# The output gate's product moved into the recurrence, and a new order of the projection's tiles

## The reference, cut to what matters

```python
z = h @ w_in + b_in
q, k, v, o, gt, ga, gb = jnp.split(z, IN_SPLITS, axis=-1)   # 256, 256, 512, 512, 16, 512, 512 wide
u = ga * jax.nn.sigmoid(gb)                                 # goes into a 31-tap convolution
...
s = jnp.einsum('bhctk,bhcsk->bhcts', qc, kc) * jnp.exp(log_d - m_t[..., None])
num = (jnp.einsum('bhcts,bhcsv->bhctv', s, vc)
       + e_int[..., None] * jnp.einsum('bhcvk,bhctk->bhctv', C_prev, qc))
h = num / jnp.maximum(jnp.abs(den), jnp.exp(-m_t))[..., None]
...
hn = h * lax.rsqrt(jnp.mean(h * h, axis=-1, keepdims=True) + EPS) * norm_g
return hn * jax.nn.sigmoid(o)                               # for the tokens alone, not the context
```

## Time and profile before

| what | value |
|---|---|
| time, median of 3 runs | 3131.33 us (3129.58 to 3132.32) |
| profiled execution: its time / its span | 3128.74 us / 3127.0 us |
| granted TensorE clock over the span | 0.915 of full |
| busy over the span | PE 2696.8 us, DVE 1746.7 us, ACT 1241.8 us, POOL 1042.4 us |

### The profile page before, as it was taken

One profiled execution on the slowest core, in us unless ns is written; L12 is line 12 of the kernel. 1 busy time (PEld: TensorE's weight loads), 2 busy tenths in 40 slices (PEclk: granted clock), 3 DMA queues, 4 the chain that ended last, 5 costly groups with the idle time before them and its releaser, 6 DMA issues. The chain is left out here.

```text
span 3127.0 us, 39919 instructions
## 1 busy us (share of the span) xinstructions
PE 2696.8 (86%) x12102; PEld 1960.0 (63%) x12103; DVE 1746.7 (56%) x2591; ACT 1241.8 (40%) x1753; POOL 1042.4 (33%) x1119
## 2 busy tenths in 40 slices
PE   5999989787679999999999939958968999965997
PEld 2455446574267877777777737745745666754776
DVE  3767767654266678677786624545462111445663
ACT  2320124520055567566665623236122111215653
POOL 0860022124444445454453421384120000105432
PEclk8999975797789999999999979979989999977999
DMA  6430010323268789899898655000202111326972
GB/s 247 148 138 1 27 54 1 139 81 131 85 230 283 241 282 318 268 311 312 268 343 253 206 159 171 7 28 2 43 14 61 41 41 42 148 115 214 311 231 46
DMA packets 162929, 472.13 MB, mean 151 GB/s; under 512 B 38637, under 2 KB 67937, under 8 KB 142073
## 3 DMA queue, kind: packets, MB, share of 16 engines
q1 hardware_dynamic: 116576, 358.25, 30.5%
q0 software_dynamic: 44704, 108.22, 15.1%
q10 hardware_dynamic: 1544, 4.33, 0.3%
HBM read 419.82 MB, written 95.81 MB: 165 GB/s over the span
## 5 line engine op out<-in xcount | busy, mean ns | idle before, releaser
L1830 PE MATMUL psum<-moe_high,moe_xg_high 128*128 128x512 f32 x960 | 390.6, 407 | 21.8 <-DVE moe_xg_low L1925 11.8
L1832 PE MATMUL psum<-moe_high,moe_xg_low 128*128 128x512 f32 x960 | 378.7, 394 | 0.0
L1831 PE MATMUL psum<-moe_low,moe_xg_high 128*128 128x512 f32 x960 | 376.1, 392 | 0.0
L1920 DVE TENSOR_TENSOR moe_low<-moe_raw,moe_high 128x2048 fp32r<-128x2048 f32 x160 | 359.2, 2286 | 13.1 <-ACT moe_high L1865 12.9
L1865 ACT ACTIVATE moe_high<-moe_raw 128x2048 fp32r<-128x2048 f32 x160 | 297.8, 1917 | 0.2 <-DMA moe_raw<-in_w_e_up 0.2
L1817 PE MATMUL psum<-moe_high_down,moe_hid_high 128*128 x488 | 204.4, 419 | 41.7 <-DVE moe_hid_low L1935 41.6
L1830 PEld LDWEIGHTS psum<-moe_high,moe_xg_high 128*128 128x128 f32 x960 | 182.1, 190 | 59.2 <-issue 24.8
L1832 PEld LDWEIGHTS psum<-moe_high,moe_xg_low 128*128 128x128 f32 x960 | 181.3, 189 | 43.1
L1831 PEld LDWEIGHTS psum<-moe_low,moe_xg_high 128*128 128x128 f32 x960 | 182.2, 190 | 36.1
L1877 ACT ACTIVATE moe_y_blk<-psum,row_w 128x1024 f32 x124 | 138.0, 1113 | 143.9 <-PE psum L1819 143.9
L1761 POOL DMA_INDIRECT moe_second<-moe_y_blk,moe_is_now x48 | 120.8, 2517 | 219.5 <-ACT moe_y_blk L1877 215.5
(11 more groups left out here) (599 smaller groups left out, 5625.1 us busy)
## 6 DMA issues: line engine op xcount, KB each, us to landing
moe_raw<-in_we_gate SPq DMA_DIRECT2D x64, 1024.0 KB
moe_raw<-in_we_up SPq DMA_DIRECT2D x64, 1024.0 KB
moe_raw<-in_we_down SPq DMA_DIRECT2D x64, 1024.0 KB
x<-in_w_ada POOLq DMA_DIRECT2D x16, 1024.0 KB
moe_raw<-in_w_e_gate SPq DMA_DIRECT2D x16, 1024.0 KB
moe_raw<-in_w_e_up SPq DMA_DIRECT2D x16, 1024.0 KB
moe_raw<-in_w_e_down SPq DMA_DIRECT2D x16, 1024.0 KB, 8.6
w_ring<-in_w_in SPq DMA_DIRECT2D x12, 1024.0 KB, 8.6
```

The lines of the kernel that those rows point to most:

```text
L1830: pe.matmul(to, x_hi, R(of_k(w_hi, k)), start=(k == 0), stop=False)
L1831: pe.matmul(to, x_hi, R(of_k(w_lo, k)), start=False, stop=False)
L1832: last = pe.matmul(to, x_lo, R(of_k(w_hi, k)), start=False, stop=(k == KD - 1))
L1920: dve.tensor_tensor(R(low[:, at:at + 2048]), raw[r][:, part], hi, ALU.subtract).then_inc(w_low, 1)
```

## The change

1. The eight `o` tiles leave the projection's plan, and with them DVE's eight additions of the bias and ACT's eight sigmoids there.
2. In the recurrence PE makes the same product in pieces, `gate_product(i)`, i = 0 to 63: one K slice of one `o` tile behind each pair's numerator and one at each pair's end. A tile thus takes four pairs and lies in bank 7. The bias is a ninth product at each tile's start (one row of ones by `b_o`). ACT copies the finished tile out (`move_gate`) and PE starts the next one behind that copy.
3. Since bank 7 is taken, the state's contribution goes to bank 1, and both scores products go to bank 0. The second waits until the first has finished, and is laid between the numerator's two products.
4. The sigmoid of `o` is taken in `stage_mix`, ahead of the silu; DVE's scaling waits for it tile by tile.
5. The projection's plan is new: all `gb`/`ga` tiles come early, mixed with `qk` and `ada`, then `gt`, and the `v` tiles last with the `gate` steps between them. `upad` is doubled, so a `ga` tile waits only for the taps of the group before the last.
6. The squares of the convolution's output go to `s.x` in place of `s.hT`, since `hT` is still needed.

```diff
 def project_plan():
     gab = lambda m, between=(): [("gb", m, 0), ("ga", m, 0), *between, ("gb", m, 1), ("ga", m, 1)]
-    plan = gab(0) + [None]
-    for i in range(0, 8, 2):
-        plan += qk[i:i + 2] + [None]
...
-    plan += [("o", t, 0) for t in range(NT)] + [("kt", t, 0) for t in range(STEPS)]
+    plan = gab(0) + [None] + qk[0:2] + [None] + gab(1, [None]) + [None] + qk[2:5] + [None] + gab(2, [None]) + qk[5:6] + [None]
+    plan += gab(3, [None]) + qk[6:] + tile("gt", *range(NT)) + tile("v", NT, NT + 1) + tile("gt", NT, NT + 1)
+    for t in range(NT):
+        plan += tile("v", t) + (tile("gate", t - 1) if 1 <= t < 5 else [])
+    plan += tile("kt", *range(STEPS))
...
-                        taps(TAPS)
+                        taps(TAPS * (n_sig // 2 - 1) - taps_done)
...
-    s.upad, s.y = sb("upad", [P, ROWS, GRID + 2 * PAD]), sb("conv_y", [P, KC, T])
+    s.upad, s.y = sb("upad", [P, 2, ROWS, GRID + 2 * PAD]), sb("conv_y", [P, KC, T])
...
+                def scores(v, i):
+                    if i == 1:
+                        pe.wait_ge(scores_done, 2 * v + 1)
+                    pe.matmul(s.bank[0][:, i * P:(i + 1) * P], s.qkT[lanes(i), 2 + k, t0:t0 + P], s.qkT[lanes(i), k, t0:t0 + P],
+                              start=True, stop=True).then_inc(scores_done, 1)
+
+                def gate_product(i):
+                    t, k = divmod(i, KD)
+                    if k == 0:
+                        if t == 0:
+                            pe.wait_ge(s.mixer_weights.ready["o"], 32)
+                        else:
+                            pe.wait_ge(o_moved, t)
+                        pe.matmul(s.bank[7][:, :], s.ones[0:1, :], s.b_o[:, :], start=True, stop=False)
+                    last = pe.matmul(s.bank[7][:, :], s.hT[:, k, t * P:(t + 1) * P], w_o[:, k], start=False, stop=(k == KD - 1))
+                    if k == KD - 1:
+                        last.then_inc(o_done, 1)
...
                         pe.wait_ge(pt_ready, v + 1)
-                        if v + 1 < NV:
-                            scores(v + 1)
                         for i in range(2):
+                            if v + 1 < NV:
+                                scores(v + 1, i)
                             last = pe.matmul(s.bank[bank + i][:, 0:W], pt[:, v % 2, i, :], s.v_aug[:, tile_of(j, d), 2 * k + i, :],
                                              start=True, stop=True)
                         last.then_inc(num_done, 1)
+                        gate_product(2 * v)
...
                         last.then_inc(local_done, 1)
+                    if v >= 0:
+                        gate_product(2 * v + 1)
...
+                def move_gate(t):
+                    act.wait_ge(o_done, t + 1)
+                    act.activation(s.sig_o[:, t, :], s.bank[7], ACT.Copy).then_inc(o_moved, 1)
...
+            for t in range(NT):
+                act.activation(s.sig_o[:, t, :], s.sig_o[:, t, :], ACT.Sigmoid).then_inc(sig_ready, 1)
```

More of the change, by code:

```diff
@@ L441, in project_plan @@
     gab = lambda m, between=(): [("gb", m, 0), ("ga", m, 0), *between, ("gb", m, 1), ("ga", m, 1)]
-    last = [entry for i, part in enumerate((("gb", 3, 0), ("ga", 3, 0), ("gb", 3, 1), ("ga", 3, 1))) for entry in (part, ("gate", i, 0))]
-    v = lambda t0, t1: [(kind, t, 0) for t in range(t0, t1) for kind in ("v", "gt")]
     qk = [("qk", m, n) for n in range(3) for m in range(4) if n < 2 or m >= 2]
-    plan = gab(0) + [None]
-    for i in range(0, 8, 2):
-        plan += qk[i:i + 2] + [None]
-    plan += qk[8:] + gab(1, [None]) + v(0, 1) + [None] + v(1, 3) + [None] + v(3, STEPS // 2) + gab(2) + v(STEPS // 2, STEPS) + last
-    plan += [("o", t, 0) for t in range(NT)] + [("kt", t, 0) for t in range(STEPS)]
+    tile = lambda kind, *tiles: [(kind, t, 0) for t in tiles]
+    plan = gab(0) + [None] + qk[0:2] + [None] + gab(1, [None]) + [None] + qk[2:5] + [None] + gab(2, [None]) + qk[5:6] + [None]
[3 more added lines that the diff above has]
+    plan += tile("kt", *range(STEPS))
     places = [i for i, entry in enumerate(plan) if entry is None]
@@ L508, in _ @@
                         pe.wait_ge(moved_a if plan[i - 8][0] in by_act else moved_v, place[i - 8])
-                    if kind in ("qk", "v", "gt", "o") and i == first[kind]:
+                    if kind in ("qk", "v", "gt") and i == first[kind]:
                         pe.wait_ge(w_ready[kind], 16 if kind == "gt" else 32)
@@ L553, in taps @@
                         w = s.convw[:, tap * KC + m:tap * KC + m + 1]
-                        rows, to = s.upad[:, :, tap:tap + GRID], s.y[:, m, :].rearrange("p (r w) -> p r w", w=GRID)
+                        rows, to = s.upad[:, m % 2, :, tap:tap + GRID], s.y[:, m, :].rearrange("p (r w) -> p r w", w=GRID)
                         if tap == 0:
@@ L587, in _ @@
                         moved = dve.tensor_tensor(s.gates[:, a, :], bank[:, 0:N_GT], b_gt[:, 0, :], ALU.add)
-                    elif kind == "o":
-                        if i == first["o"]:
-                            dve.wait_ge(later.added, 2 * later.KH * later.TILES)
-                        c.then(dve.tensor_tensor(s.sig_o[:, a, :], bank[:, :], b_o, ALU.add))
-                        c.wait(dve)
-                        moved = dve.sem_inc(moved_v, 1)
-                        dve.sem_inc(o_added, 1)
-                        continue
                     else:
@@ L611, in _ @@
                         gates.logs(dve)
-                taps(TAPS)
+                taps(TAPS * KC)
                 dve.wait_ge(gates.exps_ready, 4)
@@ L624, in _ @@
                         gates.scalar_exps(act)
-                    if kind == "o":
-                        act.wait_ge(o_added, a + 1)
-                        s.act_c.then(act.activation(s.sig_o[:, a, :], s.sig_o[:, a, :], ACT.Sigmoid))
                     if kind not in by_act:
@@ L647, in _ @@
                 c.then(pool.memset(s.v_aug[:, :, :, DV:DV + 1], 1.0))
-                pool.memset(s.upad[:, :, :], 0.0).then_inc(pads_set, 1)
+                pool.memset(s.upad[:, :, :, :], 0.0).then_inc(pads_set, 1)
                 later.load(pool)
@@ L824, in stage_mlstm @@
     N, INVERT, SCALE = 512, 0, 2 * KC + 4
-    sqy = s.hT[:, 0:KC, :]
+    sqy = s.x[:, NT // 2:NT, :]
+    w_o = s.mixer_weights.ring[:, 1]
+    local = s.bank[1][:, 0:W]
     s.rstd_y = s.hcT.rearrange("p k c -> p (k c)")[:, 1024:1024 + T]
@@ L843, in stage_mlstm @@
         y_inv, y_root, y_done, out_done = (sem(s, f"y_{x}") for x in ("inv", "root", "done", "out_done"))
+        o_done, o_moved = sem(s, "m_o_done"), sem(s, "m_o_moved")
         sq = sb("m_sq", [P, P])
@@ L882, in maxima @@
                     last.then_inc(maxima_done, 1)
-                def scores(v):
+                def scores(v, i):
                     j, d, k = pairs[P0 + v]
                     t0 = tile_of(j, d) * P
-                    for i in range(2):
-                        last = pe.matmul(s.bank[i][:, 0:P], s.qkT[lanes(i), 2 + k, t0:t0 + P], s.qkT[lanes(i), k, t0:t0 + P],
-                                         start=True, stop=True)
-                    last.then_inc(scores_done, 1)
+                    if i == 1:
[13 more added lines that the diff above has]
+                        last.then_inc(o_done, 1)
                 for n, m in halves:
@@ L909, in _ @@
                         pe.wait_ge(maxima_set, 1)
+                        scores(0, 0)
                         maxima(0)
-                        scores(0)
+                        scores(0, 1)
                     if v >= 0:
@@ L957, in _ @@
                     j, d, k = pairs[P0 + v]
+                    if v % 4 == 0 and v:
+                        move_gate(v // 4 - 1)
                     if v % 2 == 1 and v + 1 < NV:
@@ L1050, in _ @@
                         C = state[:, d, k, :]
[L1051 removed]
+                        dve.scalar_tensor_tensor(C, C, EA2[:, j, d, k:k + 1], local,
                                                  ALU.mult, ALU.add).then_inc(state_moved, 1)
```

29 lines of the change are left out of this document (16 added, 13 removed).

## The result

| | changed kernel | kernel before, same chip |
|---|---|---|
| time, median | 3147.43 us (3143.83 to 3151.70, 6 runs) | 3131.82 us (6 runs) |
| ratio | 1.0048, 95% interval 1.0035 to 1.0061 | |
| profiled execution, time / span | 3151.70 / 3150.0 us | 3128.74 / 3127.0 us |

The account below looks back on a forecast made before the run. PE was taken to bound the projection, and PE at half clock the recurrence, with the DVE and ACT round close. Projection -38, recurrence +16, mix +3.5 gave -18.5 us, 3110.2, plus 2.6: 3113 us; 8-in-10 range 3092 to 3136.

Parts of the forecast that it names:

- scores into one bank: Recurrence: the second scores product waits for the first; 0.27 us a pair, bounds 0 and 0.46.
- the slices of the gate at 0.86 us: Recurrence: 64 slices and 8 biases as products of 512 columns, 0.86 us each, 3.9 us for two pairs.
- the 2 us that I allowed for DVE's reciprocals: Recurrence: 2 us added for the pairs in which DVE also has the reciprocals.
- my upper bound of +30: Recurrence: forecast +16 us, from +5 to +30, the latter if each pair costs 0.45 more.
- the forecast's 129: Recurrence: forecast length of 129 us against 113.2 before, so +16 us.
- A: Rival: recurrence at half clock, +124 us, 3221; for a share f 114 f, f=1/3 giving 3148; chance 0.12.
- Waits at `ada`, +8: Projection: PE waits 14 us at `ada` tiles against 6.0 before, +8 us, bounds 0 and +15.
- DVE late, +9: Projection: PE waits for late DVE, mainly at the second and fourth `gate` steps; +9 us, bounds 0 and +18.
- The mix, +3.5: Mix: ACT's eight sigmoids and a table load ahead of the silus; +3.5 us, bounds 1.9 and 5.9.
- The copy of a finished tile by ACT: Recurrence: ACT's 0.7 us copy is hidden behind PE's next products, 0.3 us at worst, seven times.
- The `o` tiles, -54.9: Projection: taking the `o` tiles, 128 rows of PE, out saves 54.9 us.
- C: Rival: each recurrence pair waits for ACT or a score, +13 us; projection gives only -32; 3128 to 3134; chance 0.13.

Follow-up runs that it names:

- the last kernel: Both gate slices together at the pair's end, against the kernel with odd contributions in bank 6, mixed `gt` tiles and earlier multiplies; 3110.30 us, ratio 0.9939.
- the kernel with the recurrence alone: The changed kernel with the old plan of the projection, less its `o` tiles; ratio 1.0090 to the kernel before, recurrence 156.3 us.

## Why the prediction was wrong

**The step that failed first: "scores into one bank", 0.27 us a pair.** It measured 0.60 (0.87 against 1.47 us for scores and numerator), and against the 0.79 that the sum had for these four products, 0.68: behind a numerator stands a slice now, and there two numerator products take 0.55 and not 0.47. I had priced a lost overlap of two scores and one late weight load, and put a ceiling of 0.46 on it. No run shows the weight load's 0.15. Both the mechanism and the ceiling were wrong: the order breaks two pairs of alike products, not one. Each of the four products then costs 0.31 to 0.42 us by itself, where four in two groups cost 0.87. The kernel with two banks and the crosswise order shows that the bank, to which I tied the price, has no part in it. By the Trainium skill ("TensorE: Matmul & The Clock Gate", Part 3, the mechanism), row groups run at the same time; I had worked out a loss of up to 0.21 a pair from it, further from 0.60 than my own 0.27. What precisely the engine does between products of 64 and of 128 rows no run here shows.

**The second: the slices of the gate at 0.86 us.** That was the pace of 128 products on end. Between small ones a slice takes 0.95 or 1.06, two adjacent ones 1.81, the bias 1.05. For 64 slices and 8 biases that is 64 x 0.145 + 8 x 0.19 = 10.8 us more. The first point is 0.68 less 0.27, 32 x 0.41 = 13.1. And 20.4 us at half clock cost some 10 where I allowed 2: I had the clock come up once, and it came up after 10 us and fell three times more. Against that, a slice with maxima behind it takes 1.41 with them and not 0.95 + 0.64, in 16 pairs 2.9 less, and the 2 us that I allowed for DVE's reciprocals weren't needed. Together 27, as much as the recurrence missed by; this is an estimate from single rows. The +43 of the recurrence is also beyond my upper bound of +30. That the kernel with side-by-side scores comes to 128.3, nearly the forecast's 129, is a coincidence of two errors: in it the crosswise cost is absent and the slices cost more.

**The third: the clock in the projection, not priced at all, 16.4 us.** I had weighed the clock for the recurrence (A), and let the projection keep its 0.99. The run with the earlier multiplies takes 6.5 us of it away, 11.4 ahead of the `gt` row less 4.9 that come back from there on; the mixed `gt` tiles take 8.0 away. The two don't add (9.9 and 8.4 us remain over 274.0 with the one or the other, 8.2 with both). The Trainium skill (the same page, Part 1) says that idle stretches bring the throttle back; here the rows agree for the wait of 3.74, behind which 13.90 us become 16.88, and not for the one of 2.80, behind which they stay 13.90. I had cited that rule for the recurrence only, where PE doesn't idle, and not for the waits of 2 to 3 us that I was forecasting in the same text. Its other half, that activity releases the throttle, the rows contradict if activity is what the profile calls busy: 133.00 of 133.00 us at 0.50.

**Waits at `ada`, +8:** right in mechanism and nearly in size, 16.3 us in six waits against the 14 of the forecast.

**DVE late, +9:** wrong, 0.3 us. DVE kept its forecast time (281 and 280.2 at the last `qk`), PE didn't. Even with PE 22 us earlier, behind the earlier multiplies, no such wait is seen: 29 taps beside POOL took 1.86 us on the average in the changed kernel, not 1.99, and PE's own slow `gt` row gave DVE time. Only one execution, that of the last kernel, shows a part of it, 4.1 us; what differed there stays open. The two errors of the projection, +9 too many and 16 forgotten, are of opposite signs.

**The mix, +3.5:** measured +2.6. The copy of a finished tile by ACT: hidden, as forecast. The `o` tiles, -54.9: right, as the kernel with the recurrence alone shows (-55.4).

**The rivals.** A was wrong as it stood: the clock in the recurrence rose from 0.55 to 0.93, and without the gate's product it stays at 0.50. The forecast of this was right, but for the three falls on the way. In A's own working 114 f with f = 1/3 gives 3151, not 3148; the share at half clock was 0.13. C named the right stage, but gave it waits; there are none. The slower side was held by A only, and so the case that came had no chance of its own: a recurrence that is PE's own time and longer than the sum of rows from other neighbourhoods.

## What to carry to other kernels

A duration holds for an instruction among its neighbours: take it start to start from a row with the same products on both sides, and before an order is changed, look at which alike products stand side by side and are parted. On an engine whose list is in order, a small job (a multiply) that must be early for another engine belongs ahead of any move that waits for a third; one place earlier was worth 24 us here, the sign of the whole change. And a wait of about 3 us on PE can cost as much again in the clock behind it (3.0 us behind one of 3.74, nothing behind one of 2.80).

## What the runs showed that I had not expected

- PE at 133.00 of 133.00 us busy with products of 128 and 129 columns and the maxima stays at 1.2 GHz; with two more products of 512 columns in each pair the mean is 0.93 to 0.97 of 2.4. Yet in the kernel before, a stretch of the same small products, side by side and with PE busy for only 4.23 of 6.50 us, was granted the full clock: PE's busy share doesn't tell the clock.
- 128 products of 16 columns in a row, with no idle time recorded, lower the clock (0.72 over that stretch); in pairs of tiles they nearly did not in one kernel (3.64 us for two, one fall of the clock behind the first two) and did in another (4.15 to 4.53). Why there, stays open.
- Two chips ran the same kernel before at 3102.8 and 3132.1 us, 0.9% apart. In the kernels profiled on them, what lies behind the mix took 2529 to 2535 us on the one and 2553 to 2566 on the other, while the projection of the new plan took 307.1 and 307.2 us on the one and 304.2 to 312.1, mostly 307, on the other.
